# Conditioning sums on VectorE, a reordered layer head, and causal attention outputs with the values as stationary operand

## The chip, the core and the metric

The kernel runs on one core of one Trainium2 chip. The metric is the device time of one execution in microseconds, lower is better. The core's engines are TensorE (PE, its weight loads PEld), VectorE (DVE), ScalarE (ACT), GpSimd (POOL) and SyncE (SP), which here issues the weight DMAs.

## The reference

One sequence of 256 positions and 1024 channels passes two blocks. The first has two transformer layers conditioned on a vector `c` (a matrix-vector product with `ada_w`, six vectors of 1024 each layer), with differential attention, neighbourhood attention and a convolutional feed-forward network. The second has two hybrid layers, and most of the change is there:

```python
def hybrid_layer(x, ...):
    h = rmsnorm_2(x, norm_g)
    proj = h @ w_in                       # nsa_q, nsa_kv, pool_in, conv_in, fox_qkv, gates, merges ...
    o_nsa = nsa_mixer(...)                # gated sum of compressed, selected and window attention, 4 heads of 64
    o_pool = pool_mixer(...)
    o_conv = conv_mixer(...)
    o_fox = fox_mixer(...)                # causal attention with a decay from a cumulative sum, 4 heads of 64
    for i, o in enumerate((o_nsa, o_pool, o_conv, o_fox)):
        branch = (o * silu(gates[:, :, i])) @ w_branch[i]
        acc += sigmoid(merge[:, :, i]) * branch
    return x + acc @ w_out
```

With 256 positions, the selection takes every block and the window covers all keys, so the selected and the window parts are plain causal attention over different keys.

## The kernel before

**Weights.** All weights pass one queue of units of up to 1 MB. SP loads a unit into one of three slots of `RAW` (`load_unit`). ACT makes its high part (`split_hi`, L526), DVE or POOL its low part (`split_lo`/`lo_prep`, L536), and TensorE multiplies in three products (L554 to L556; L963 to L965, L970 and L971, L918 to L924 with activations stationary). `NH`/`NL` (NHL in the trace) hold the parts of the normed input, `WHL` those of the weights. PE, DVE, ACT, POOL and SP each run their own instruction list, written out by hand, and meet through semaphores.

**Conditioning.** A unit of `ada_w` is 128 rows by 2048 columns and isn't split: `pe_ada` (L568) multiplies it in float32 with a stationary operand of 32 columns (`CB`, which holds silu(c) and silu(c_ctx)), four matmuls beside each other on four column groups. Each float32 matmul is two recorded passes, so a unit shows as x8. Blocks 0 to 7 of units are named `("ada", b, k)`. Block 4 goes another way: DVE adds its eight units up, each times its element of `c`, in `WSUM` (`dve_ada_step`, L579), and TensorE sums over the partitions once (`pe_ada_joint`, L586).

**Hybrid layer.** `pe_layer` is the order on PE: `pe_head` (norm and the first projections, among them the values `va`, `vb`), the up projections of the compression, the gate projections g1, g2, g0, g3 with `pe_compress_sum` (L2116) and the first score jobs between, and then the causal attention in six jobs i = 0 to 5 (`CAUSAL`: fox, queries 0 to 127 and 128 to 255; then the two NSA kinds likewise). A job goes: `pe_causal_qk` scores (L2205, L2206, L2208), DVE mask and maximum (L2221, L2225, L2228), ACT exponential with row sums (L2253), DVE reciprocal r (L2234) and for NSA r times the gate (L2238), PE transpose (`pe_causal_turn`, L2273), ACT copy (L2283), `pe_causal_pv` (L2298), and DVE scaling by r into `OF` or `ON` (`dve_causal_out`, L2310). A projection of about 5.8 us stands between a job's steps on PE. At the end `pe_turn_nsa` and `pe_turn_fox` transpose `ON` and `OF` (L2602, L2615), and DVE multiplies by the gate `G` (`dve_gated`, L2431).

**Head.** `dve_turn_product` is a lane shuffle (L1957) and a multiplication by the rotary table (L1959); L2051 is the cumulative sum of the decay, on which ACT's `act_decay` (L2004, L2006) waits.

Of the kernel before, what the change touches and what calls it, by code (L numbers as in the profile page):

```python
# [13 lines left out]
P = 128  # L14
# [123 lines left out]
UP_ADA = {("up", 0, 0): (0, 1, 2, 3), ("up", 0, 2): (4,), ("up", 0, 3): (5,), ("up", 0, 4): (6,), ("up", 0, 5): (7,)}  # L138
QKV_ADA = {("qkv", 1, 4): (0, 1, 2), ("qkv", 1, 5): (3,)}
JOINT_ADA = {("up", 0, HALF_FT + 1): (7,)}  # L140
# [9 lines left out]
def unit_orders():  # L150
# [32 lines left out]
    for j in range(HALF_FT):  # L183
        add(("up", 0, j), 2)
        for k in {1: range(4), 2: (4,), 3: (5,), 4: (6,), 5: (7,)}.get(j, ()):
            add_ada(3, k)
# [109 lines left out]


# [67 lines left out]
def bass_two_block_decoder(nc, wstream, first, small, consts, late, rpb, xin, out):  # L365
    ctx = ExitStack()
    with ctx:
# [47 lines left out]
        QN, KN, KC, QF, KF, CBG, ON, OF = (  # L415
            sb(n, [P, 2, 256]) for n in ("QN", "KN", "KC", "QF", "KF", "CBG", "ON", "OF"))
# [53 lines left out]
        c_silu, c_zero, lam_v, lam_exp = (sem(n) for n in ("c_silu", "c_zero", "lam_v", "lam_exp"))  # L470
# [101 lines left out]
        def dve_ada_step(e, k):  # L572
            v = UNIT_OF["ada", 4, k]
            e.wait_ge(d_raw[v % 3], 16 * (v // 3 + 1))
            if k == 0:
                e.tensor_scalar(WSUM[:, :], RAW[:, v % 3, :], CB[:, k, 0:1], None, ALU.mult).then_inc(ada_acc, 1)
                return
            e.wait_ge(ada_acc, k)
            e.scalar_tensor_tensor(out=WSUM[:, :], in0=RAW[:, v % 3, :], scalar=CB[:, k, 0:1], in1=WSUM[:, :],  # L579
                                   op0=ALU.mult, op1=ALU.add).then_inc(ada_acc, 1)  # L580

        def pe_ada_joint(e):
            e.wait_ge(ada_par, 3)
            e.wait_ge(ada_acc, 8)
            for j in range(4):
                mm = e.matmul(AB[32 * j:32 * j + 32, :], ONE.to_broadcast([P, 32]), WSUM[:, 512 * j:512 * j + 512],  # L586
                              start=True, stop=True)
# [341 lines left out]
        def pe_wide(e, key, outs, T, xh, xl, wait_x):  # L929
# [3 lines left out]
            for j, o in enumerate(outs):  # L933
# [655 lines left out]
        def pe_ffn(e, l):  # L1589
            T, ring = (512, 3) if l == 0 else (256, 6)  # L1590
            for c, js in chunks(l):
                for jj, j in enumerate(js):
# [6 lines left out]
                    if l == 0 and c == 0:  # L1599
                        for k in UP_ADA.get(("up", 0, jj), ()):  # L1600
                            if k > 1:
                                pe_ada(e, 3, k)
                        if jj == 9:
                            pe_ada_turn(e, 3)
                    if l == 0 and c == 1 and jj == 1:
                        pe_ada_joint(e)
# [242 lines left out]
        def pe_proj(e, l, name):  # L1849
            pe_ring_free(e, l, name)  # L1850
# [1519 lines left out]
```

## Time and profile before

| | |
|---|---|
| median of 3 runs | 1594.96 us (1594.63 to 1595.36) |
| the profiled execution | 1595.22 us, its span 1593.4 us |
| mean granted clock of TensorE | 0.997 |
| PE / PEld busy | 98% / 82% |
| DVE / ACT / POOL busy | 59% / 47% / 34% |
| first hybrid layer, second | about 1075 to 1330 us, 1330 to 1582 us |

The span is what the profile covers; the rest of the execution's 1595.22 us, 1.8 us, lies around it. A row of a timeline gives start, duration, engine, line, operation and operands; rows that follow each other closely are joined as xN, and a matmul's duration reaches past the start of the next one, so the cost of matmuls is read from start to start.

### The profile page before, as it was taken

The page shows a single profiled execution, that of the slowest core. Times are in us where ns is not written, and L with a number is a line of the kernel's source. Part 1 is how long each engine was busy: PE and PEld are TensorE (multiplying, and loading weights), DVE is VectorE, ACT ScalarE, POOL GpSimd, SP SyncE. Part 2 cuts the span into 40 slices and gives each one's busy share as a digit, 9 for nine tenths or more (in the row PEclk, how much of TensorE's full clock was granted, in tenths as well). Part 3 has the DMA queues.
Part 4 walks back from the last instruction along what each step waited for, and adds up shares of the span by engine and source line. Part 5 has one row for each costly group of instructions (what it writes and reads, how often), then busy time and mean ns, then how long its engine had stood idle before and what let it go on. Part 6 is the DMA issues. An engine that isn't in the chain of part 4 may idle for free.

```text
span 1593.4 us, 23097 instructions
## 1 busy us (share of the span) xinstructions
PE 1568.6 (98%) x9146; PEld 1303.4 (82%) x9146; DVE 936.4 (59%) x1441; ACT 750.5 (47%) x1360; POOL 543.3 (34%) x354
## 2 busy tenths in 40 slices
PE   8999999999999999999999999999999999999998
PEld 5778557778887888879768899989998889998887
DVE  4434485555575554342266888757876457968435
ACT  5324485444322433243375755445654445654444
POOL 2224243322211222212273111007424657623663
PEclk9999999999999999999999999999999999999999
DMA  9264500534174222364313754454534534633551
GB/s 393 94 246 187 212 30 9 204 135 157 63 268 184 80 81 73 124 207 164 123 37 113 267 192 172 162 190 170 183 133 161 199 143 171 215 133 132 185 211 54
DMA packets 52603, 249.17 MB, mean 156 GB/s; under 512 B 20624, under 2 KB 21008, under 8 KB 26256
## 3 DMA queue, kind: packets, MB, share of 16 engines
q1 hardware_dynamic: 43744, 243.90, 42.2%
q10 hardware_dynamic: 8752, 3.80, 1.0%
q8 instruction: 73, 1.20, 0.3%
q14 instruction: 34, 0.28, 0.0%
HBM read 246.63 MB, written 1.05 MB: 155 GB/s over the span
## 4 chain that ended last, share of the span: by engine, by line
PE 88%; DVE 5%; ACT 3%; issue 1%; DMA 1%; POOL 1%; SPq 0%; POOLq 0%; ACTq 0%; DVEq 0%
PE psq L554 16%; PE psq L555 16%; PE psq L556 16%; PE ps L554 7%; PE ps L556 7%; PE ps L555 7%; PE psq L970 3%; PE ps L568 1%; PE psq L971 1%; PE ps L970 1%; DMA RAW<-wstream 1%; ACT WHL L526 1%; PE psq L1365 1%; PE ps L1393 1%; PE psq L2298 1%
## 5 line engine op out<-in xcount | busy, mean ns | idle before, releaser
L536 DVE TENSOR_TENSOR WHL<-RAW,WHL 128x1024 fp32r<-128x1024 f32 (+3 forms) x264 | 324.9, 1254 | 290.1 <-ACT WHL L526 289.6
L536 POOL TENSOR_TENSOR WHL<-RAW,WHL 128x1024 fp32r<-128x1024 f32 (+2 forms) x116 | 304.5, 2627 | 504.6 <-ACT WHL L526 471.8
L526 ACT ACTIVATE WHL<-RAW 128x1024 fp32r<-128x1024 f32 (+2 forms) x380 | 361.4, 1002 | 196.1 <-DMA RAW<-wstream 98.6
L554 PE MATMUL psq<-NHL,WHL 128*128 128x256 f32 (+1 forms) x1072 | 353.8, 330 | 1.7 <-POOL WHL L536 0.7
L555 PE MATMUL psq<-NHL,WHL 128*128 128x256 f32 (+1 forms) x1072 | 349.0, 326 | 0.0
L556 PE MATMUL psq<-NHL,WHL 128*128 128x256 f32 (+1 forms) x1072 | 348.9, 325 | 0.0
L554 PEld LDWEIGHTS psq<-NHL,WHL 128*128 128x128 f32 x1072 | 205.2, 191 | 28.9 <-issue 7.5
L556 PEld LDWEIGHTS psq<-NHL,WHL 128*128 128x128 f32 x1072 | 205.3, 191 | 16.6
L555 PEld LDWEIGHTS psq<-NHL,WHL 128*128 128x128 f32 x1072 | 205.3, 191 | 15.4
L554 PE MATMUL psq<-WHL,NHL 128*128 128x512 f32 (+1 forms) x320 | 124.8, 390 | 1.7 <-DVE WHL L536 1.7
L556 PE MATMUL psq<-WHL,NHL 128*128 128x512 f32 (+1 forms) x320 | 123.3, 385 | 0.0
L555 PE MATMUL psq<-WHL,NHL 128*128 128x512 f32 (+1 forms) x320 | 123.2, 385 | 0.0
L554 PE MATMUL ps<-NHL,WHL 128*128 128x512 f32 (+1 forms) x272 | 94.9, 349 | 0.0
L555 PE MATMUL ps<-NHL,WHL 128*128 128x512 f32 (+1 forms) x272 | 94.1, 346 | 0.0
L556 PE MATMUL ps<-NHL,WHL 128*128 128x512 f32 (+1 forms) x272 | 94.0, 346 | 0.0
L1716 DVE SCALAR_TENSOR_TENSOR TMP<-psq,SMALL,TMP 128x510 f32<-128x510 f32 (+1 forms) x64 | 39.2, 613 | 79.7 <-ACT TMP L1677 79.7
L699 ACT ACTIVATE TMP<-X 128x256 f32<-128x256 f32 (+1 forms) x52 | 25.1, 498 | 120.7 <-DVE X L1532 59.9
L1677 ACT ACTIVATE TMP<-psq,SMALL 128x512 f32<-128x512 f32 (+1 forms) x64 | 40.8, 666 | 87.0 <-PE psq L556 87.0
L554 PEld LDWEIGHTS psq<-WHL,NHL 128*128 128x128 f32 x320 | 60.1, 188 | 14.3 <-DVE WHL L536 2.1
L556 PEld LDWEIGHTS psq<-WHL,NHL 128*128 128x128 f32 x320 | 60.1, 188 | 11.5
L555 PEld LDWEIGHTS psq<-WHL,NHL 128*128 128x128 f32 x320 | 60.1, 188 | 11.0
L1752 POOL TENSOR_TENSOR HL<-TMP,HH 128x512 fp32r<-128x512 f32 x22 | 28.8, 1308 | 112.9 <-ACT HH L1663 112.9
(389 smaller groups left out, 2975.6 us busy)
## 6 DMA issues: line engine op xcount, KB each, us to landing
RAW<-wstream SPq DMA_DIRECT2D x194, 1024.0 KB, 4.8
RAW<-wstream SPq DMA_DIRECT2D x32, 704.0 KB, 4.0
K<-first SPq DMA_DIRECT2D x4, 1024.0 KB, 17.2
RAW<-wstream SPq DMA_DIRECT2D x4, 800.0 KB, 4.3
X<-xin SPq DMA_DIRECT2D x2, 1024.0 KB, 6.1
V<-first SPq DMA_DIRECT2D x2, 1024.0 KB, 19.3
Q<-first SPq DMA_DIRECT2D x2, 1024.0 KB, 24.7
BR<-rpb ACTq DMA_DIRECT2D x8, 256.0 KB, 8.2
```

The costliest lines, as they stand in the source:

```text
L526: e.activation(WH[:, u % 3, a:z], RAW[:, v % 3, a:z], ACT.Copy).then_inc(w_hi, 1)
L536: e.tensor_tensor(WL[:, u % 3, a:z], RAW[:, v % 3, a:z], WH[:, u % 3, a:z].bitcast(F32), ALU.subtract).then_inc(w_lo_p if pool else w_lo_v, 1)
L554: e.matmul(o, lh, rh, start=start, stop=False)
L555: e.matmul(o, lh, rl, start=False, stop=False)
L556: return e.matmul(o, ll, rh, start=False, stop=stop)
L568: mm = e.matmul(AB[32 * j:32 * j + 32, :], CB[:, c, :], RAW[:, v % 3, 512 * j:512 * j + 512], start=k == 0, stop=k == ada_units(b) - 1)
L699: e.activation(sq_tile(n, m), X[:, m, 0:NORM_T[n]], ACT.Square).then_inc(x_sq, 1)
L970: e.matmul(o[:, 0:512], wh, x, start=start, stop=False, skip_group_check=True)
L971: return e.matmul(o[:, 0:256], wl, x[:, 0, :], start=False, stop=stop, skip_group_check=True)
L1677: e.activation(acc_tile(l, U, s), up_banks(l, jj)[s][:, :], ACT.Identity, scale=small_at("fconv", (3 * l + 1) * 44 + j + FT * s), bias=sma ...
L1716: e.scalar_tensor_tensor(out=a3[:, :, 1:256], in0=o3[:, :, 0:255], scalar=w(0), in1=a3[:, :, 1:256], op0=ALU.mult, op1=ALU.add).then_inc(u ...
L1752: e.tensor_tensor(HL[l][:, jj, :], acc_tile(l, U, 0), HH[l][:, jj, :].bitcast(F32), ALU.subtract).then_inc(h_lo, 1)
```

## The change

1. **Conditioning.** Units 4 to 7 of block 3 are no longer multiplied on PE. DVE sums them for both vectors (`WSUM` gets two planes), in steps ahead of up projections 1, 3, 5 and 7, and `pe_ada_joint(3)` multiplies the two sums before up 8. Their loads follow up 2, 4, 6 and 8 instead of 2 to 5. Unit (5, 3) is multiplied before qkv 4 of layer 1 and not before qkv 5. `CB` is cleared by POOL and not by DVE.
2. **Head.** DVE's split of the first value unit (`lo_prep(qn)`) moves into the norm, after its step m = 3. The shuffle of `dve_turn_product` stands apart from its product, and the product now follows the split of the first g1 unit. ACT's copy to `KF` follows that unit's high part. The first half of g2 stands ahead of `pe_causal_qk(0)`, the second behind it.
3. **Causal outputs.** DVE scales P by r ahead of the transpose (`dve_causal_scale`), `pe_causal_turn` waits for that. `pe_causal_pv` has the values as stationary operand, 64 columns on the left or right column half of PE, and P^T moves: the result is already transposed. NSA's kinds and the compressed part are summed in one bank by accumulation. `ON`, `OF`, their transposes and the scaling of outputs go away.
4. **Gating.** `dve_fox_gated` reads the fox result ahead of `dve_pool_sums`, `dve_nsa_gated` after conv's taps; `conv_u` stands ahead of `cmp_weigh(0)`, and r of the compressed part is multiplied by its gate.

```diff
-UP_ADA = {("up", 0, 0): (0, 1, 2, 3), ("up", 0, 2): (4,), ("up", 0, 3): (5,), ("up", 0, 4): (6,), ("up", 0, 5): (7,)}
-QKV_ADA = {("qkv", 1, 4): (0, 1, 2), ("qkv", 1, 5): (3,)}
+UP_ADA = {("up", 0, 0): (0, 1, 2, 3)}
+UP_SUMMED = {1: 4, 3: 5, 5: 6, 7: 7}
+QKV_ADA = {("qkv", 1, 4): (0, 1, 2, 3)}
...
+            for c, t in enumerate(sums):
...
+                e.scalar_tensor_tensor(out=t, in0=RAW[:, v % 3, :], scalar=CB[:, k, c:c + 1], in1=t,
+                                       op0=ALU.mult, op1=ALU.add).then_inc(ada_acc, 1)
...
+        def dve_causal_scale(e, l, i):
...
+            for g, tile in enumerate(p_tiles(qt)):
+                p = TMP[:, tile, :].rearrange("p (l k) -> p l k", l=2)
+                e.tensor_tensor(p, p, r[:, g, :].unsqueeze(2).to_broadcast([P, 2, 256]), ALU.mult).then_inc(p_scaled, 1)
...
         def pe_causal_pv(e, l, i):
...
-            o = bank[2][:, 256 * (i % 2):256 * (i % 2) + 256]
-            for n, h in enumerate(HEADS):
-                for k in range(qt + 1):
-                    c = ((n % per) * (qt + 1) + k) * P
-                    v = VF[:, k, 64 * h:64 * h + 64] if kind == 2 else VN[:, k, 64 * kind:64 * kind + 64]
-                    mm = e.matmul(o[:, 64 * h:64 * h + 64], TMP[:, t_tiles(qt)[n // per], c:c + P], v, start=k == 0,
-                                  stop=k == qt)
+            if i == 2:
+                e.wait_ge(z_mul, z_value(l, 3))
+            for k in range(qt + 1):
+                for a in range(2 if kind == 2 else 1):
+                    for par in range(2):
+                        half = slice(64 * par, 64 * par + 64)
+                        o = bank[2][half, :].rearrange("p (c q) -> p c q", c=2)[:, :, qt * P:qt * P + P]
+                        t = TMP[:, t_tiles(qt)[par if qt else 0], :].rearrange("p (n q) -> p n q", n=4)
+                        t = t[:, k:4:2, :] if qt else t[:, 2 * par:2 * par + 2, :]
+                        if kind == 2:
+                            v, o, t = VF[:, k, 128 * a + 64 * par:128 * a + 64 * par + 64], o[:, a, :], t[:, a, :]
+                        else:
+                            v = VN[:, k, 64 * kind:64 * kind + 64]
+                        mm = e.matmul(o, v, t, start=i in (0, 2) and k + a == 0, stop=kind == 2 and k == qt,
+                                      skip_group_check=True)
...
@@ pe_layer @@
             pe_compress_sum(e, l)
+            pe_proj(e, l, "g2", (0,))
             pe_causal_qk(e, l, 0)
-            pe_gates(e, l, 2)
+            pe_proj(e, l, "g2", (1,))
```

In the order on DVE the head of a hybrid layer reads before, from the split of the last compression unit on:

```order
L536 TENSOR_TENSOR WHL<-RAW,WHL 128x1024 [waits w_hi]
L1957 STREAM_SHUFFLE TMP<-TMP 128x512 [waits raw_copy]
L1959 TENSOR_TENSOR TMP<-TMP,LATEC 128x512 [waits nrot_v]
L536 TENSOR_TENSOR WHL<-RAW,WHL 128x1024 [waits w_hi]
L2051 SCALAR_TENSOR_TENSOR TMP<-CONST,psq 128x256 [waits fx_tr]
L1966 TENSOR_TENSOR QN<-QN,TMP 128x512 [waits nrot_c,nrot_v]
```

And now (L548 is the split, L1986 the shuffle, L1992 the product, L2083 the cumulative sum):

```order
L548 TENSOR_TENSOR WHL<-RAW,WHL 128x1024 [waits w_hi]
L1986 STREAM_SHUFFLE TMP<-TMP 128x512 [waits raw_copy]
L548 TENSOR_TENSOR WHL<-RAW,WHL 128x1024 [waits w_hi]
L1992 TENSOR_TENSOR TMP<-TMP,LATEC 128x512 [waits nrot_v]
L2083 SCALAR_TENSOR_TENSOR TMP<-CONST,psq 128x256 [waits fx_tr]
L1999 TENSOR_TENSOR QN<-QN,TMP 128x512 [waits nrot_c,nrot_v]
```

The split of the first g1 unit has passed the product, and the product stands directly ahead of the cumulative sum. On DVE around the two jobs that precede the pool's sums (L2459) it read before:

```order
L536 TENSOR_TENSOR WHL<-RAW,WHL 128x1024 [waits w_hi]
L2234 RECIPROCAL STAT<-STAT 128x4 [waits att_exp]
L2238 TENSOR_TENSOR STAT<-STAT,CM 128x4 [waits att_r,gs_v]
L2310 TENSOR_TENSOR OF<-psq,STAT 128x256 [waits att_r,att_pv]
L2221 TENSOR_TENSOR psq<-psq,LATEC 128x512 [waits att_qk]
L2225 TENSOR_REDUCE STAT<-psq 128x2x2 [waits att_mask]
L536 TENSOR_TENSOR WHL<-RAW,WHL 128x1024 [waits w_hi]
L2459 TENSOR_TENSOR PU<-PU 128x2x256 [waits pads,sb_copy]
```

And now (L2270 and L2274 are r, L2291 the scaling, L2257 and L2261 mask and maximum, L2460 the gating, L2488 the pool's sums):

```order
L548 TENSOR_TENSOR WHL<-RAW,WHL 128x1024 [waits w_hi]
L2270 RECIPROCAL STAT<-STAT 128x4 [waits att_exp]
L2274 TENSOR_TENSOR STAT<-STAT,CM 128x4 [waits att_r,gs_v]
L2291 TENSOR_TENSOR TMP<-TMP,STAT 128x512 [waits att_r]
L2291 TENSOR_TENSOR TMP<-TMP,STAT 128x512
L2257 TENSOR_TENSOR psq<-psq,LATEC 128x512 [waits att_qk]
L2261 TENSOR_REDUCE STAT<-psq 128x2x2 [waits att_mask]
L548 TENSOR_TENSOR WHL<-RAW,WHL 128x1024 [waits w_hi]
L2460 TENSOR_TENSOR TMP<-psq,G 128x512 [waits g_v,att_pv]
L2488 TENSOR_TENSOR PU<-PU 128x2x256 [waits pads,sb_copy]
```

The output scaling of a job became two scalings of P of twice the width, on which the job's transposes wait, and a gating that waits for the second fox output stands ahead of the pool's sums.

## Rows read from the trace of the kernel before

**Rows 1.** The page, busy time of each engine over the span.
```profile
PE 1568.6 (98%) x9146; PEld 1303.4 (82%) x9146; DVE 936.4 (59%) x1441; ACT 750.5 (47%) x1360; POOL 543.3 (34%) x354
```

**Rows 2.** Timeline of the weight loads in the head, layer 0.
```profile
1094.03 0.19 PEld L965 LDWEIGHTS psq<-NHL,WHL 128*128 128x128 f32 x1
1095.26 0.19 PEld L554 LDWEIGHTS psq<-WHL,NHL 128*128 128x128 f32 x1 [1.03 <-DVE WHL L536]
```

**Rows 3.** Timeline of PE where projection g1 changes halves.
```profile
1121.22 0.28 PE L556 MATMUL psq<-NHL,WHL 128*128 128x256 f32 x1
1121.98 0.39 PE L554 MATMUL psq<-NHL,WHL 128*128 128x256 f32 x1 [0.48 <-POOL WHL L536]
```

**Rows 4.** Timeline of DVE in the head, layer 0.
```profile
1091.07 1.94 DVE L867 TENSOR_TENSOR NHL<-TMP,NHL 128x256 fp32r<-128x256 f32 x1 [1.20 <-ACT NHL L849]
...
1094.22 0.98 DVE L536 TENSOR_TENSOR WHL<-RAW,WHL 128x800 fp32r<-128x800 f32 x1
...
1116.42 2.12 DVE L1959 TENSOR_TENSOR TMP<-TMP,LATEC 128x512 f32<-128x512 f32 x1
```

**Rows 5.** Timeline of PE around the compression's sums and causal_qk(0).
```profile
1126.49 1.06 PE L2116 MATMUL ps<-CONST,TMP 32*128 32x16 f32 x8
...
1129.82 0.41 PE L556 MATMUL psq<-NHL,WHL 128*128 128x256 f32 x1
1130.04 0.41 PE L554 MATMUL psq<-NHL,WHL 128*128 128x256 f32 x1
...
1132.59 0.28 PE L554 MATMUL psq<-NHL,WHL 128*128 128x256 f32 x1
1132.71 0.28 PE L555 MATMUL psq<-NHL,WHL 128*128 128x256 f32 x1
```

**Rows 6.** Windows there and in the second layer: busy us, granted clock, DMA share, GB/s.
```profile
1130.00:1135.00 5.00, 5.00 (x35) 5.00 (x34) 4.63 (x11) 0.34 (x2) 0.56 (x1) 0.74 0.74 251
1385.00:1390.00 5.00, 5.00 (x32) 5.00 (x31) 4.41 (x10) 0.36 (x2) 0.54 (x1) 0.66 0.69 247
```

**Rows 7.** Timeline of PE, causal outputs of job 1.
```profile
1168.51 1.90 PE L2298 MATMUL psq<-VNF,TMP 128*128 128x64 f32 x16
1170.24 1.04 PE L2273 MATMUL ps<-CONST,TMP 128*128 128x128 f32 x8
```

**Rows 8.** Timeline of PE, attention of the layer before; half-width stationaries.
```profile
809.95 1.09 PE L1393 MATMUL ps<-TMP,V 128*64 128x128 f32 x16
810.98 1.13 PE L1365 MATMUL psq<-K,Q 64*128 64x512 f32 x4
```

**Rows 9.** Timeline of PE, one conditioning unit of block 3.
```profile
367.77 0.39 PE L556 MATMUL psq<-NHL,WHL 128*128 128x512 f32 x1
368.08 1.07 PE L568 MATMUL ps<-RAW,CB 128*32 128x512 f32 x8
369.08 0.50 PE L554 MATMUL ps<-NHL,WHL 128*128 128x512 f32 x1
369.42 0.39 PE L555 MATMUL ps<-NHL,WHL 128*128 128x512 f32 x1
```

**Rows 10.** Source view of the running weight sums.
```profile
L579 DVE SCALAR_TENSOR_TENSOR WSUM<-RAW,CB,WSUM x7: 2345/2349/3192, 440.2 to 482.4; 128x2048 f32<-128x2048 f32 x7
```

**Rows 11.** Timeline of PE, output transposes.
```profile
1249.92 0.60 PE L2602 MATMUL psq<-CONST,ON 128*128 128x128 f32 x4
1250.27 0.48 PE L554 MATMUL psq<-WHL,NHL 128*128 128x512 f32 x1
```

**Rows 12.** Timeline of PE at the next layer's first projection.
```profile
686.42 1.06 PE L568 MATMUL ps<-RAW,CB 128*32 128x512 f32 x8
688.17 0.47 PE L918 MATMUL psq<-NHL,WHL 128*128 128x512 f32 x1 [0.69 <-ACT NHL L851]
```

**Rows 13.** Timeline of DVE between two causal jobs.
```profile
1162.06 2.06 DVE L2238 TENSOR_TENSOR STAT<-STAT,CM 128x4 f32<-128x4 f32 x1
...
1165.10 0.69 DVE L2225 TENSOR_REDUCE STAT<-psq 128x4 f32<-128x512 f32 x1
```

More of the change, by code:

```diff
@@ L184, in unit_orders @@
         add(("up", 0, j), 2)
-        for k in {1: range(4), 2: (4,), 3: (5,), 4: (6,), 5: (7,)}.get(j, ()):
+        for k in {1: range(4), 2: (4,), 4: (5,), 6: (6,), 8: (7,)}.get(j, ()):
             add_ada(3, k)
@@ L231, in unit_orders @@
             runs[r:r] = [("ada", b, k) for k in ks]
+    for key, b in JOINT_AT.items():
+        r = runs.index(key)
+        runs[r:r] = [("joint", b)]
     return keys, every, runs
@@ L295, in product_end @@
     return GEMM_BEFORE[KEYS[v]] + unit_products(KEYS[v])
+ADA_ACC = {}
+acc_count = 0
+for b_, ks_ in SUMMED.items():
+    for k_ in ks_:
+        acc_count += 1 if b_ == 4 else 2
+        ADA_ACC["ada", b_, k_] = acc_count
 SPLIT_UNITS = [v for v, k_ in enumerate(KEYS) if k_[0] != "ada"]
@@ L582, in pe_ada_joint, with weight_sums, dve_ada_step @@
[L582 to L587, printed above, removed]
+        def weight_sums(b):
+            return [WSUM[:, c, :] for c in range(1 if b == 4 else 2)]
+        def dve_ada_step(e, b, k):
+            v = UNIT_OF["ada", b, k]
+            sums = weight_sums(b)
+            at = ADA_ACC["ada", b, k] - len(sums)
+            e.wait_ge(d_raw[v % 3], 16 * (v // 3 + 1))
+            if b == 4 and k == 0:
+                e.wait_ge(gemm, product(("joint", 3)))
+            for c, t in enumerate(sums):
+                if k == SUMMED[b][0]:
+                    e.tensor_scalar(t, RAW[:, v % 3, :], CB[:, k, c:c + 1], None, ALU.mult).then_inc(ada_acc, 1)
+                    continue
+                e.wait_ge(ada_acc, at - len(sums) + c + 1)
+                e.scalar_tensor_tensor(out=t, in0=RAW[:, v % 3, :], scalar=CB[:, k, c:c + 1], in1=t,
+                                       op0=ALU.mult, op1=ALU.add).then_inc(ada_acc, 1)
@@ new lines, in bass_two_block_decoder, with pe_ada_joint @@
+        CBF = CB[:, :, :].rearrange("p k n -> p (k n)")
+        ONE_AT = (CBF[:, 16:48], CBF[:, 15:47])
+        def pe_ada_joint(e, b):
+            if b == 4:
+                e.wait_ge(ada_par, 3)
+            e.wait_ge(ada_acc, ADA_ACC["ada", b, SUMMED[b][-1]])
+            for c, t in enumerate(weight_sums(b)):
+                for j in range(4):
+                    mm = e.matmul(AB[32 * j:32 * j + 32, :], ONE_AT[c], t[:, 512 * j:512 * j + 512], start=b == 4,
+                                  stop=b == 4 or c == 1)
@@ L588, in pe_ada_joint @@
             mm.then_inc(gemm, 1)
         def act_ada_row(e, b):
-            e.wait_ge(gemm, product(("ada", b, ada_units(b) - 1)))
+            e.wait_ge(gemm, product(("joint", b) if b in SUMMED else ("ada", b, ada_units(b) - 1)))
             if b >= 2:
@@ L1599, in pe_ffn @@
                     if l == 0 and c == 0:
-                        for k in UP_ADA.get(("up", 0, jj), ()):
-                            if k > 1:
-                                pe_ada(e, 3, k)
+                        if jj == 0:
+                            pe_ada(e, 3, 2)
+                            pe_ada(e, 3, 3)
+                        if jj == 8:
+                            pe_ada_joint(e, 3)
                         if jj == 9:
@@ L1707, in dve_ffn @@
                     U, key = 22 * l + j, ("up", l, j)
+                    if l == 0 and j in UP_SUMMED:
+                        dve_ada_step(e, 3, UP_SUMMED[j])
                     split_lo(e, ahead(key), False)
@@ L2379, in act_cmp_turn, with pe_cmp_pv @@
             e.activation(TMP[:, 6, 128 * qt:128 * qt + P], bank[6 + qt][:, 0:P], ACT.Copy).then_inc(att_pt, 1)
-        def pe_cmp_pv(e, l, qt):
-            e.wait_ge(att_pt, TR_BASE + 11 * l + 10 + qt)
-            e.matmul(bank[3 + qt][:, 0:256], TMP[:, 6, 128 * qt:128 * qt + P], VCB, start=True,
-                     stop=True).then_inc(att_pv, 1)
-        def dve_cmp_out(e, l, qt):
-            x = TMP[:, 8 + qt, 256:512]
-            g = GS[:, qt, 0:4].unsqueeze(2).to_broadcast([P, 4, 64])
-            e.wait_ge(att_pv, PV_BASE + 8 * l + 7 + qt)
-            e.wait_ge(gs_v, l + 1)
-            e.tensor_tensor(x.rearrange("p (h d) -> p h d", h=4),
-                            bank[3 + qt][:, 0:256].rearrange("p (h d) -> p h d", h=4), g, ALU.mult).then_inc(att_o, 1)
-            e.wait_ge(att_o, O_BASE + 8 * l + 6 + 2 * qt)
-            e.wait_ge(nsa_o, 4 * l + 2 * qt + 1)
-            e.tensor_tensor(ON[:, qt, :], ON[:, qt, :], x, ALU.add).then_inc(nsa_o, 1)
+        def pe_cmp_pv(e, l):
+            e.wait_ge(att_pt, TR_BASE + 11 * l + 11)
+            for c in range(2):
+                mm = e.matmul(bank[2][:, 256 * c:256 * c + 256], VCB[:, P * c:P * c + P], TMP[:, 6, 0:256], start=False,
+                              stop=True, skip_group_check=True)
+            mm.then_inc(att_pv, 1)
         GATE_ORDER = (1, 2, 0, 3)
@@ L2890, in act_layer @@
             act_causal_exp(e, l, 5)
+            act_gated(e, l, 3, FOX_Z)
             act_conv_b(e, l)
```

192 lines of the change are left out of this document (79 added, 113 removed).

## The prediction

> **What bounds the kernel.** I read the page's busy times first: PE works 98% of the span, 24.8 of 1593.4 us are left over, and DVE, ACT and POOL are far from full [rows 1]. So an edit gains by passes taken off PE, by closing one of PE's few gaps, or by the clock, and work given to another engine costs nothing unless PE comes to wait for it. Then I read the timelines where the change puts its hand. PE stands in the head of a hybrid layer for the low half of the first value unit: one weight load starts at 1094.03, the next at 1095.26, where 0.12 us is usual, 1.1 us lost; DVE's split, for which it waits, starts only at 1094.22 [rows 2, 4]. PE stands again in g1, for POOL's half of the split: 1121.22 to 1121.98, 0.64 us over a step [rows 3]. The clock is the third place. Behind the compression's sums and the first scores the projection matmuls start 0.22 us apart, at 1132.59 the step is 0.12 again, and the windows grant 0.74 and 0.66 [rows 5, 6]. Those are the two levels, 1.2 and 2.4 GHz. What PE did just before, from 1126.49 on, is matmuls with 32 or 64 rows and few columns [rows 5].
>
> **Conditioning.** Four units leave PE. One takes 1.00 us to the next start, and the changes of form around it cost 0.31 and 0.34 us where two 512-column steps take some 0.23 each: 0.19 more, 1.19 in all [rows 9]. 4 x 1.19 = 4.8 us go. The joint product has twice a unit's passes, 2 x 1.00, with the changes once: about 2.1. Gain 2.7 us. On DVE come eight operations of 128x2048 at 2.35 us [rows 10], 19 us in four up steps' pairs, while DVE works 59% of the span [rows 1]; the low splits queued behind them are made ahead of their products. I take nothing for this; if cover were missing at each of the four steps, each would cost up to its 4.7 us less the slack of a unit, so I allow 0 to 4 us. Unit (5, 3) fills a wait: PE stands from the end of the first three units, 687.48, to 688.17 [rows 12]. It costs 1.19 where it stood, and about 0.7 of its time falls into the wait, so I take 0.5, with 0 to 0.9 as bounds, since its weights may land late there. Clearing `CB` is nothing: its first matmul waits for data.
>
> **Head.** The value split of 0.98 us goes ahead of a norm step where DVE waited 1.20 us [rows 4]; it fits, and up to 1.1 us of the gap closes if ACT's half has come by then. In g1 the high part comes one copy earlier, about 0.5 us, which covers most of the 0.64. Against it stands the cumulative sum: before, the split lay between the product and the sum, so that the product (1116.42, 2.12 us) was long done. Now the product stands after the split and directly ahead of the sum. Beside POOL's split it took 2.12 us, where a reduction of 128x512 takes 0.69 [rows 4, 13]. The sum may start up to 2 us later, ACT's decay, the g2 split and the copy for `compress_sum` with it. I take 0.6 us gained for each layer, 1.2 in all, bounds -0.5 and 1.5 each. The Trainium skill, "SBUF — State Buffer", section "SBUF: two separate sides", says that a DVE operation with two SBUF inputs and a GpSimd one that reads SBUF lock each other out for a whole instruction; the 2.12 us agree. By it each moved product could double the loss, and it is why I don't take the full 1.5.
>
> **Clock.** With g2's first half, 24 dense matmuls of 0.12 us, 2.9 us, between the 16-column sums and the 64-row scores [rows 5], the two thin stretches no longer join. The loss is read from the windows: 0.34 x 5 = 1.7 us in the second layer; in the first the slow steps reach from 1129.82 at the latest to 1132.59, at least 2.8 us at half clock, so 1.4 or more, and I take 1.7 there too [rows 5, 6]. Gain 3.4 us if the dips go, 0 if they stay.
>
> **Causal outputs.** Before, 16 passes take 1.73 us, 0.108 each [rows 7]; a layer has 3 jobs of 8 and 3 of 16, 72 passes, 7.8 us, 15.6 in both. After, fox has 24 passes of 128 columns on half-width stationaries. The nearest row has just this form: 16 passes in 1.03 us, 0.064 each [rows 8], less than the 0.108 of one that has the array alone, so the halves run side by side. 24 x 0.064 = 1.55 us. The NSA kinds have 24 passes of 256 columns. Two steps of four 512-column passes take 1.00 us [rows 9], so a step of 256 columns 0.25, and a pair of halves as much: 12 x 0.25 = 3.0 us. Entering the narrow form costs 0.08 [rows 9] for each of six jobs, 0.5. Together 5.1 us a layer; gain 2.7, for both 5.4. Bounds: if a step ran at half of four-abreast, twice as long, the NSA part would lose 3.0 more a layer (the rival below), and if leaving the form were free it would gain 1 more for both. The 16 transposes go: 0.35 us for four [rows 11], and about 0.1 for the change of form, as behind the conditioning unit [rows 9]: 4 x 0.43 = 1.7 us.
>
> The first stands against a rule. The Trainium skill, "TensorE: Matmul & The Clock Gate", section "The mechanism", says that weight loads overlap matmuls in flight only where row groups differ, and here both halves use all rows. By it each pair would run one after the other, and the gain of 5.4 would be a loss. The trace has the pairing with all 128 rows [rows 8] and contradicts it, so I follow the row.
>
> **Scaling of P.** New on DVE: nine 128x512 operations a layer, two in a job of 256 keys, on the path exponential, r, scale, transpose, copy, output. Their nearest rows are 0.69 us for 512 columns of DVE [rows 13] and 2.12 for a product beside POOL [rows 4]. Job 1: r's second operation runs 1162.06 to 1164.12 [rows 13], the transposes start at 1170.24 [rows 7]. Two scalings end between 1165.5 and 1168.4. That leaves 1.8 us or more, so I take nothing. Queued behind them are mask and maximum, which ended at 1165.79 [rows 13] and would end at 1170 in the bad case; the exponential and the next scaling then still have a projection and more ahead of them. The output scalings, which left, and `conv_u` ahead of the weighing I price at nothing.
>
> **Sum.** 2.7 + 0.5 + 1.2 + 3.4 + 5.4 + 1.7 = 14.9 us. From the profiled execution's own 1595.2 that is 1580.3; the median of the runs is 0.3 lower, so I forecast 1580.0.
>
> **Rivals.**
> *The half clock stays*, at the same place or behind g2's second half: the thin matmuls are all still there, and only their spacing changed. For it speaks that the scores still follow each other in one piece; against it that every job has such scores and the span's mean grant of 0.997 leaves 4.8 us for all dips, of which these two are 3.4. 1580.0 + 3.4 = 1583.4.
> *The halves don't pair* at 256 columns or in accumulation in one bank: each NSA pass costs 0.22 and not 0.125, 24 x 0.1 x 2 layers = 4.6 more, and 0.108 for fox, 2.1 more: 1586.7. Against it stand [rows 8].
> *DVE comes late in the head*: the cumulative sum's delay reaches `compress_sum`, and the gains in the head turn into a loss of 1 to 2 us a layer: 1583 to 1585.
> *Slower than before*: the scalings at 2.1 us each, with masks and low splits behind them, push the exponential past the next job's slack, so that PE waits at the transposes. It decides once job 1's scalings end 1.8 us later than the bad case above. To eat 15 us, the ten turns of jobs 1 to 5 of both layers must each wait 1.5 us; at 2 us each the kernel ends at 1600. Against it: DVE waits for ACT before these splits and has time between jobs.
>
> **Numbers.** My forecast has 0.5; the clock staying 0.2; DVE late in the head or a smaller new wait 0.15; halves unpaired 0.07; a larger gain, by terms at their upper bounds, 0.05; slower 0.03. The forecast's own range is 1577.5 to 1582; the whole runs from 1576.5 to 1586. What this measurement can tell from no change is 0.2%, 3.2 us. Only a heavy form of the DVE rivals or the last ends above 1591.8: faster 0.95, same 0.02, slower 0.03.
>
> **What would show it.** Causal outputs: 16 passes of 128 columns to the next start in 1.0 us, 8 passes of 256 columns in about 1.0. Windows behind g2 at 1.00. PE's gap for the value unit under 0.5 us, no gap at g1's second half, and none at the 16-column sums. No PE wait on DVE's scaling at a transpose. In the up projections of layer 0 no wait for DVE's low splits. I am wrong if a row of 0.5 us or more of PE idle names DVE scaling, DVE's weighted sums or the copy for the sums, or if half-clock steps of 0.21 us remain.

## The result, and the profile after

The changed kernel took 1597.84 us (median of 14 runs, 1595.97 to 1600.28), the kernel before beside it 1594.98 (14 runs). The ratio is 1.0016, with a 95% interval of 1.0009 to 1.0023: slower by 0.16%, where 1580.0 was forecast. That is 12 us above the top of the forecast range, 1576.5 to 1586. Its profiled execution has a span of 1596.9 us and a granted clock of 0.994.

The page, busy times and the chain that ended last, to be read against [rows 1]:

```profile
PE 1566.0 (98%) x9066; PEld 1295.0 (81%) x9066; DVE 951.3 (60%) x1446; ACT 748.7 (47%) x1360; POOL 536.7 (34%) x356
...
PE 80%; DVE 10%; ACT 5%; issue 2%; DMA 2%; POOL 0%; SPq 0%; ACTq 0%; POOLq 0%; DVEq 0%
```

PE's busy time is down by 2.6 us, with matmuls at half clock counted at their full length, and it is still busy 98% of a longer span. The chain says more: PE's share of it is 80%, DVE's 10 and ACT's 5, where before it was 88, 5 and 3. A timeline of PE in the first layer, outputs 1, 2 and 3 with the transposes of jobs 3, 4 and 5 behind them, for [rows 7], and then job 5's transposes in the second layer:

```profile
1164.53 1.09 PE L2352 MATMUL psq<-TMP,VNF 128*64 128x128 f32 x16
1165.55 1.09 PE L2322 MATMUL ps<-CONST,TMP 128*128 128x128 f32 x8
...
1173.59 0.65 PE L2352 MATMUL psq<-TMP,VNF 128*64 128x256 f32 x4
1175.88 0.66 PE L2322 MATMUL ps<-CONST,TMP 128*128 128x128 f32 x4 [1.65 <-DVE TMP L2287]
...
1186.62 1.08 PE L2352 MATMUL psq<-TMP,VNF 128*64 128x256 f32 x8
1187.63 1.09 PE L2322 MATMUL ps<-CONST,TMP 128*128 128x128 f32 x8
```

```profile
1444.12 1.97 PE L2322 MATMUL ps<-CONST,TMP 128*128 128x128 f32 x8 [2.68 <-DVE TMP L2291]
```

The matmul form does what was forecast: 16 passes of 128 columns take 1.02 us to the next start, for 1.73. Output 1 starts 4.0 us earlier than before, output 2 (before at 1178.12) begins 4.5 us earlier. Then PE stands 1.65 us for DVE's scaling of job 4 (L2287), in the second layer 1.63 us for job 4 and 2.68 us for job 5. Behind the stand at 1175 and the one at 1444 the clock is at its lower level, 1.2 GHz, for much of the time. The windows (us, busy time by engine, granted clock, DMA) answer [rows 6]:

```profile
1130.00:1135.00 5.00, 5.00 (x43) 4.53 (x42) 4.64 (x14) 2.25 (x10) 0.00 (x0) 1.00 0.62 210
1175.00:1180.00 5.00, 4.06 (x21) 3.76 (x22) 2.86 (x6) 3.01 (x10) 0.00 (x0) 0.72 0.38 159
1180.00:1185.00 5.00, 5.00 (x29) 5.00 (x29) 4.39 (x5) 2.40 (x4) 2.46 (x1) 0.60 0.00 0
1385.00:1390.00 5.00, 4.99 (x40) 4.70 (x42) 4.63 (x9) 0.23 (x1) 0.98 (x1) 1.00 0.67 252
1440.00:1445.00 5.00, 2.32 (x16) 1.59 (x15) 4.76 (x10) 0.00 (x0) 0.73 (x1) 0.84 0.59 210
1445.00:1450.00 5.00, 4.94 (x19) 4.11 (x18) 3.60 (x10) 3.11 (x5) 1.70 (x1) 0.50 0.01 3
1450.00:1455.00 5.00, 5.00 (x16) 3.96 (x15) 3.63 (x10) 2.15 (x3) 1.60 (x3) 0.63 0.56 208
```

At the old places, 1130 and 1385, the clock is now full. At the new ones it is 0.72, 0.60, 0.84, 0.50 and 0.63. What is missing to 1, times 5 us, comes to 3.4 us in the first layer and 5.1 in the second, the most that this can have cost. The timeline of DVE in the first layer, for [rows 13]:

```profile
1161.99 2.10 DVE L2274 TENSOR_TENSOR STAT<-STAT,CM 128x4 f32<-128x4 f32 x1
1164.12 1.29 DVE L2291 TENSOR_TENSOR TMP<-TMP,STAT 128x512 f32<-128x512 f32 x2
...
1166.06 0.69 DVE L2261 TENSOR_REDUCE STAT<-psq 128x4 f32<-128x512 f32 x1
1169.33 1.23 DVE L548 TENSOR_TENSOR WHL<-RAW,WHL 128x1024 fp32r<-128x1024 f32 x1 [2.58 <-ACT WHL L538]
...
1171.07 2.31 DVE L2488 TENSOR_TENSOR PU<-PU 128x512 f32<-128x512 f32 x1
...
1175.14 0.69 DVE L2287 TENSOR_TENSOR TMP<-TMP,STAT 128x512 f32<-128x512 f32 x1
```

The low split (L548) that DVE made at 1168.36 before it makes at 1169.33 now, though PE is 4 us ahead, and job 4's scaling comes at 1175.14. Where the lead went is read from output 3. Rows of the kernel before, transposes of job 4, output 3 and transposes of job 5:

```profile
1178.96 0.61 PE L2273 MATMUL ps<-CONST,TMP 128*128 128x128 f32 x4
...
1186.57 1.90 PE L2298 MATMUL psq<-VNF,TMP 128*128 128x64 f32 x16
1188.30 1.04 PE L2273 MATMUL ps<-CONST,TMP 128*128 128x128 f32 x8
```

Output 3 starts at 1186.62 now, 0.05 us later than before. Of the 4.5 us of lead the wait for the scaling took about 1.5, the half clock behind it the other 3. The chain of waits between 1155 and 1190, first of the kernel before, then of the changed one, shares by line:

```profile
by line: PE psq L554 22.9%; PE psq L556 21.2%; PE psq L555 21.2%; PE psq L2298 14.7%; PE ps L2273 7.6%; PE psq L2208 3.9%; PE psq L2331 3.3%; PE ps L2208 3.0%; PE ps L2331 2.4%; issue 0.4%
```

```profile
by line: ACT TMP L2302 12.8%; ACT WHL L538 11.2%; DVE STAT L2274 10.5%; issue 8.9%; DVE TMP L2291 7.4%; DVE WHL L548 7.1%; DVE X L2499 7.1%; DVE PU L2488 6.4%; DVE STAT L2264 4.0%; DVE TMP L2287 4.0%; DVE ps L2257 2.0%; DVE X L2503 2.0%; DV
```

Before, every piece of it is PE, but for 0.4% of issue. Now it runs ACT exponential (L2302), ACT high part (L538), DVE low split (L548), the pool's sums and means (L2488, L2499), r and gate (L2274), scaling (L2291), mask and maximum, and the next exponential. None of its 106 pieces is PE's: in this stretch the loop closed without a wait for PE.

### The profile page after: what moved, and what is told of

The parts are those of the page before. It is cut to its first block, busy times and chain, and to the rows that moved or that the text cites. A ratio compares the mean times of both kernels' runs of the same rounds, so it can differ in the third digit from the quotient of the medians.

```text
span 1596.9 us, 22916 instructions
## 1 busy us (share of the span) xinstructions
PE 1566.0 (98%) x9066; PEld 1295.0 (81%) x9066; DVE 951.3 (60%) x1446; ACT 748.7 (47%) x1360; POOL 536.7 (34%) x356
## 4 chain that ended last, share of the span: by engine, by line
PE 80%; DVE 10%; ACT 5%; issue 2%; DMA 2%; POOL 0%; SPq 0%; ACTq 0%; POOLq 0%; DVEq 0%
PE psq L566 14%; PE psq L568 14%; PE psq L567 14%; PE ps L566 7%; PE ps L568 7%; PE ps L567 7%; PE psq L996 3%; DMA RAW<-wstream 2%; DVE WHL L548 2%; ACT WHL L538 2%; PE psq L997 1%; PE ps L996 1%; PE ps L580 1%; PE psq L1391 1%; ACT TMP L2302 1%
## 5 line engine op out<-in xcount | busy, mean ns | idle before, releaser
L548 DVE TENSOR_TENSOR WHL<-RAW,WHL 128x1024 fp32r<-128x1024 f32 (+3 forms) x264 | 333.8, 1288 | 295.5 <-ACT WHL L538 294.5
L548 POOL TENSOR_TENSOR WHL<-RAW,WHL 128x1024 fp32r<-128x1024 f32 (+2 forms) x116 | 298.2, 2573 | 503.9 <-ACT WHL L538 471.1
L538 ACT ACTIVATE WHL<-RAW 128x1024 fp32r<-128x1024 f32 (+2 forms) x380 | 361.2, 1002 | 190.7 <-DMA RAW<-wstream 88.2
```

What stands on the lines that cost most here:

```text
L538: e.activation(WH[:, u % 3, a:z], RAW[:, v % 3, a:z], ACT.Copy).then_inc(w_hi, 1)
L548: e.tensor_tensor(WL[:, u % 3, a:z], RAW[:, v % 3, a:z], WH[:, u % 3, a:z].bitcast(F32), ALU.subtract).then_inc(w_lo_p if pool else w_lo_v, 1)
```

## The experiments

Medians, and the ratio to the kernel before beside them with its interval. Before was 1595.33 to 1595.87 in these comparisons. The intervals are some 2 us wide to either side, so the order of e8 to e15 among themselves is mostly inside them; what is said of it rests on the profiles, one for each kernel.

| kernel | us | ratio |
|---|---|---|
| e1 no causal part | 1597.82 | 1.0009 (1.0000 to 1.0017) |
| e2 causal part alone | 1599.63 | 1.0029 (1.0018 to 1.0040) |
| e3 pool's sums later | 1594.93 | 0.9997 (0.9988 to 1.0006) |
| e4 low splits later | 1585.32 | 0.9935 (0.9923 to 0.9948) |
| e5 before, low splits later | 1593.26 | 0.9984 (0.9975 to 0.9992) |
| e6 e1, low splits later | 1588.20 | 0.9953 (0.9940 to 0.9967) |
| e7 waits filled | 1598.78 | 1.0022 (1.0013 to 1.0030) |
| e8 e4, g2 whole | 1584.97 | 0.9934 (0.9922 to 0.9947) |
| e9 e4, two more moves | 1583.82 | 0.9926 (0.9913 to 0.9938) |
| e10 e9, g2 whole | 1583.78 | 0.9925 (0.9913 to 0.9937) |
| e11 e4, no conditioning part | 1588.11 | 0.9953 (0.9940 to 0.9967) |
| e12 e4, no head part | 1583.06 | 0.9922 (0.9910 to 0.9935) |
| e13 e12, value split moved | 1582.99 | 0.9918 (0.9905 to 0.9932) |
| e14 e12, copy and product moved | 1586.63 | 0.9941 (0.9928 to 0.9953) |
| e15 e13, conv_u moved | 1582.70 | 0.9913 (0.9899 to 0.9926) |

**e1: the causal part undone.** The changed kernel with the parts 3 and 4 of the diff taken back.

> The kernel before with the conditioning and head parts alone, causal outputs and gating as before. Theory A (PE, now ahead, waits for DVE's scaling at the turns of jobs 4 and 5, and the stall brings the half clock): the trace of after is 3.1 us ahead at the start of the hybrid layers, and about 1.0 and 1.6 us more are gained up to the first turn of each layer, so 1594.98 - 5.7 = about 1589.3, half-clock stretches at most where before had them. Rival B (the earlier parts only moved waits and give nothing): 1594 to 1595. Rival C (DVE and ACT are the bound of the causal stretch anyway, so that even without scaling PE's lead is lost there): 1591 to 1593.

The median of 1597.82 is above all three forecasts. In mechanism it is C: PE is 4.7 us ahead of the kernel before at output 2, and by 1197 all is gone. The waits of PE, us in total, times, longest:

```profile
PE psq L2335 <- DVE ON L2350: 2.8, 2, 1.9
...
PE psq L567 <- DVE CXY L2551: 2.4, 2, 1.2
```

There is no scaling of P here. PE waits for the old scaling of outputs (`ON`) and for `CXY`, and behind these waits the window at 1190 has a clock of 0.66. So the lead is lost to DVE without the new scaling, and the scaling is not the only cause.

**e2: the causal part alone.**

> The kernel before with the new causal outputs and gating alone. Theory A: PE reaches job 4's turn about 4 us later than in the changed kernel, while DVE's scaling comes at the same time, so the waits are gone or under 0.5 us and no half clock follows; the form of the matmuls and the transposes that went give 2 to 5 us: 1590 to 1593. Rival D (the new matmul form itself brings waits or the half clock): slower than before by 3 us or more, with half-clock stretches behind the outputs.

Theory A's sum missed. The waits for DVE's scaling are there although PE lacks the 3 us of the conditioning part:

```profile
PE ps L2285 <- DVE TMP L2254: 3.9, 2, 2.7
...
PE ps L2285 <- DVE TMP L2250: 1.7, 2, 1.1
```

No half clock stands behind the first scores. In the first layer it follows the wait of 2.67 us at job 5, in the second one of only 0.57 us at job 4 (0.75 at 1435). In number, and in its dips, this is rival D; that the form alone doesn't bring the half clock only e4 shows, which has the form and full clock. I had taken the lead as the cause; the loop had also become longer. From one low split to the next, around job 3, DVE took 7.72 us in the kernel before and 8.76 in the changed one.

**e3: the pool's sums behind job 5's maximum.**

```diff
             dve_fox_gated(e, l)
-            dve_pool_sums(e, l)
             dve_causal_r(e, l, 4)
             dve_causal_scale(e, l, 4)
             dve_causal_max(e, l, 5)
+            dve_pool_sums(e, l)
```

> The changed kernel with the pool's sums on DVE moved behind the scaling and the maximum of jobs 4 and 5. Theory A: the wait of 1.65 us at job 4's turn in each layer goes, and with it the half clock behind it in the first layer (some 3 us); in the second layer the wait at job 5 shrinks: 1588 to 1592. Rival D (the form of the matmuls brings the half clock): the waits go, 3.3 us, but the dips stay: about 1594 to 1595. Rival C: the time saved comes back as a wait at job 5, 1596 or more.

The wait at job 4 went. One of 2.1 us stands at job 5 in each layer, with the half clock behind it: part of what was taken came back one job later, as C had it. The 1594.93 falls into D's range, but D had these waits gone.

**e4: the low splits behind the maximum.**

```diff
             dve_causal_max(e, l, 3)
-            lo_prep(e, l, "pool", False)
             dve_causal_r(e, l, 3)
             dve_causal_scale(e, l, 3)
             dve_causal_max(e, l, 4)
-            lo_prep(e, l, "conv_x", False)
+            lo_prep(e, l, "pool", False)
             dve_fox_gated(e, l)
-            dve_pool_sums(e, l)
             dve_causal_r(e, l, 4)
             dve_causal_scale(e, l, 4)
             dve_causal_max(e, l, 5)
+            lo_prep(e, l, "conv_x", False)
+            dve_pool_sums(e, l)
+            dve_causal_r(e, l, 5)
+            dve_causal_scale(e, l, 5)
             lo_prep(e, l, "conv_b", False)
             dve_pool_means(e, l)
-            dve_causal_r(e, l, 5)
-            dve_causal_scale(e, l, 5)
```

> As e3, and DVE's low splits of the pool, conv_x and conv_b units also stand behind scaling and maximum of their job, so that DVE no longer waits for ACT's high part between a job's exponential and its scaling. Theory A, with the DVE and ACT ping-pong as the cause: scaling ends some 3 us earlier in each job, no wait at any turn, no dip: 1585 to 1588. If the low splits were what PE needs next, a wait for them appears at the projections and the time is no better than e3.

As expected, 12.5 us below the changed kernel, by order alone. Timelines of DVE, of POOL, and of PE at output 2:

```profile
1167.53 2.14 DVE L2274 TENSOR_TENSOR STAT<-STAT,CM 128x4 f32<-128x4 f32 x1
1169.71 0.69 DVE L2287 TENSOR_TENSOR TMP<-TMP,STAT 128x512 f32<-128x512 f32 x1
...
1172.45 1.22 DVE L548 TENSOR_TENSOR WHL<-RAW,WHL 128x1024 fp32r<-128x1024 f32 x1
...
1176.22 3.38 DVE L2291 TENSOR_TENSOR TMP<-TMP,STAT 128x512 f32<-128x512 f32 x2 [0.23 <-DVE STAT L2274]
```

```profile
1176.07 2.37 POOL L548 TENSOR_TENSOR WHL<-RAW,WHL 128x1024 fp32r<-128x1024 f32 x1 [6.42 <-ACT WHL L538]
```

```profile
1174.57 0.65 PE L2352 MATMUL psq<-TMP,VNF 128*64 128x256 f32 x4
1175.15 0.66 PE L2322 MATMUL ps<-CONST,TMP 128*128 128x128 f32 x4
```

Job 4's scaling ends at 1170.4, 4.7 us ahead of the transposes, and the low split at 1172.45 finds ACT's high part ready. Two scalings of job 5, started beside POOL's low split of 1176.07, take 3.38 us instead of 1.29, 2.1 more, and still nobody waits. The Trainium skill, in "SBUF — State Buffer", section "SBUF: two separate sides", has a lock between a DVE operation with two SBUF inputs and a GpSimd one that reads SBUF; the trace agrees: the pair ends at 1179.60, 1.16 us after POOL's end at 1178.44, about the 1.29 us that it takes alone.

**e5 and e6: the same order without the new outputs.** e5 is the kernel before, e6 is e1, both with reciprocal and maximum of jobs 2 to 5 ahead of the low splits.

> The kernel before with DVE's order alone changed as in e4: reciprocal and maximum of jobs 2 to 5 ahead of the low splits of the pool, conv_x and conv_b units. Theory A (before, PE and the DVE-ACT chain of these jobs are about level, PE sets the end): nothing to gain while PE carries its old work, 1594.5 to 1595.5, no wait of PE gone that was there. Rival E (the order by itself is worth most of e4's gain): 1588 to 1591.

> e1 (conditioning and head parts, old causal outputs) with the order of e4 on DVE. Theory A: in e1 PE was 4.7 us ahead before the waits on ON and CXY and lost all; with the order it keeps it in both layers: 1594.98 - 3.1 - 1.0 - 1.6 - up to 1 of the half clock = 1588.5 to 1589.5; e4 stands 3 to 5 us below it, and that is what the matmul form and the transposes give. Rival C (the chain is as long without the order): no better than e1.

e6 is A's case to 0.3 us, with e4 2.9 us below it instead of 3 to 5. e5 gained 2.1 us where A said nothing. Its profile has only one of before's two half-clock stretches behind the scores (about 1.5 us), and its PE timeline agrees with that of before to 0.36 us up to 1211. Its runs step with the granted clock: 1592.0 to 1592.5 us at 1.000, 1593.2 to 1593.6 at 0.998 and 0.999, 1594.5 and 1595.1 at 0.997. The kernel before gets nothing from a higher clock: beside e5, its five runs at 0.999 took 1595.05 to 1595.46, its four fastest, at 0.998, 1594.55 to 1594.80. So the order alone is worth 0.4 us on PE's timeline and up to 2.1 in the time, where more clock comes with it (why is open), and 10 to 12 us once PE is faster (e1 to e6, and the changed kernel to e4). The new outputs are worth e6 less e4, 2.9 us.

**e7: PE's waits filled.** 12 dense matmuls ahead of the wait at job 4, 20 at job 5 of the second layer.

```diff
+            fill = 12 if i == 4 else 20 if i == 5 and l else 0
+            if fill:
+                e.wait_ge(att_pt, base)
+                for n in range(fill):
+                    e.matmul(bank[6][:, 0:256], NH[:, n % DT, 0:P], NH[:, n % DT, 0:256], start=True, stop=True)
```

> The changed kernel with dense matmuls of 128 rows and 256 columns, whose result nobody reads, put in front of PE's wait for the scaled P: 12 at job 4's turn in both layers, 20 at job 5's in the second. Theory H (PE's idle stretch, followed by thin matmuls, brings the half clock): the half-clock stretches at 1175 to 1185 and 1440 to 1455 go, worth 3.4 + 5.1 us, and the waits' own time stays: 1589 to 1592. Rival I (the thin matmuls alone bring it): dips as in the changed kernel, 1597 to 1600.

The time missed H and fell into I's range, while the windows are H's:

```profile
1175.00:1180.00 5.00, 4.93 (x39) 4.44 (x38) 2.77 (x6) 3.09 (x10) 0.00 (x0) 1.00 0.36 151
1180.00:1185.00 5.00, 4.62 (x39) 3.88 (x37) 4.47 (x5) 2.32 (x4) 2.49 (x1) 1.00 0.07 8
1190.00:1195.00 5.00, 4.94 (x15) 4.05 (x15) 4.35 (x11) 2.36 (x4) 2.49 (x2) 0.50 0.06 10
1445.00:1450.00 5.00, 4.85 (x33) 3.81 (x31) 3.53 (x11) 1.49 (x3) 0.00 (x0) 1.00 0.43 177
```

```profile
1187.30 1.11 PE L2327 MATMUL ps<-CONST,TMP 128*128 128x128 f32 x4 [2.68 <-DVE TMP L2291]
```

At 1175, 1180 and 1445, where the fill is, the clock is full, and the second layer's causal stretch takes 2.4 us less. In the first layer PE now reaches job 5 at full speed and waits there 2.68 us, where I had put no fill; behind that wait the clock is 0.50, and this layer's stretch takes 2.5 us more. Half clock on PE had given DVE time to catch up. Taking it away up to job 5 moved the wait and gained nothing: the transposes of job 5 start at 1187.30 where they started at 1187.63. Up to there the loop sets the time; behind job 5 the clock counts as well.

**e8: g2 whole again, on e4.**

> e4 with both halves of projection g2 behind causal_qk(0), as before the change. Theory J (the prediction's term: the spacing keeps the clock): half-clock windows come back after the first scores, 1.7 us in each layer, so e4 + 2 to 4 us: 1587.5 to 1589. Rival K (the dips depend on something else that is gone too): same as e4 within 1 us.

Both half-true. The half clock is back in both layers:

```profile
1125.00:1130.00 5.00, 5.00 (x31) 4.89 (x31) 4.96 (x5) 1.59 (x3) 2.37 (x1) 0.68 0.62 213
1375.00:1380.00 5.00, 4.94 (x31) 4.73 (x31) 4.97 (x4) 3.11 (x5) 3.75 (x2) 0.74 0.47 159
```

And the time is e4's. In the first layer the stretch from the sums to job 0's transposes takes 17.9 us in e4 and 18.0 in e8. Splitting g2 brings two more changes of form (6.4 us of g2 for 5.86), and PE, being faster, meets this in e4:

```profile
1141.05 0.66 PE L2322 MATMUL ps<-CONST,TMP 128*128 128x128 f32 x4 [0.55 <-DVE TMP L2287]
```

**e9 and e10: two more moves, with g2 in halves and whole.** Job 0's r and scaling stand ahead of `dve_gates(2)`, and `conv_u` ahead of the low split of `conv_c`.

> e4 with two more moves on DVE: reciprocal and scaling of job 0 ahead of the low split of the g2 unit's follower, and conv_u ahead of the low split of conv_c. In e4 PE waited 0.57 us at job 0's turn in the first layer, and about 0.46 and 0.4 us for CXY. Theory A: these go, e4 less 1.0 to 1.5 us: 1583.8 to 1584.5. If the moved splits become late instead, no gain.

> e9 with g2 whole behind causal_qk(0). In e8 the half clock came back (1.7 us a layer), and the whole took no longer, since the split of g2 had cost two changes of form (0.55 us a layer) and a wait at job 0's turn (0.7 and 0.2 us). With that wait gone in both kernels, the split should now pay: this one 1 to 2.5 us slower than e9. If the half clock's cost is hidden by something else still, equal.

e9 met A. In its trace the wait at job 0 is gone and one of 1.5 us at job 1's transposes, for ACT's copy, has come. e10 pays for its half clock and waits there only 0.7 us: equal again, against my expectation.

**e11 and e12: conditioning, and head, undone on e4.**

> e4 with the conditioning as before. From the traces PE was 3.1 us ahead at the first hybrid layer through it: e4 + 2.7 to 3.3 us, 1588 to 1588.6. If part of it were hidden elsewhere, less than 2 us.

> e4 with the head as before: value split, product order, KF copy, g2 whole. Seen in the traces: the value unit's gap of 1.0 us returns in both layers, the half clock of 1.7 us too, against changes of form and a wait of together 0.75 to 1.25 us a layer: e4 + 2.5 to 3.5 us: 1587.8 to 1588.8. If the head moves gained only the value gap: e4 + 2.

The conditioning part is worth 2.8 us, as expected. Without the head part I had expected 2.5 to 3.5 us more, and e12 is 2.3 us faster than e4. The stretch from the sums to job 0's transposes takes 16.2 us in both layers of its trace, where e4 takes 17.9 and 17.3, which is more than the value unit's gap of 1.0 us costs. Two windows of e12, whose like is half slow in e8:

```profile
1125.00:1130.00 5.00, 4.94 (x41) 4.73 (x41) 4.71 (x8) 0.42 (x2) 2.48 (x1) 1.00 0.75 233
1375.00:1380.00 5.00, 4.94 (x41) 4.73 (x41) 4.88 (x6) 0.60 (x3) 2.72 (x1) 1.00 0.66 215
```

The matmuls behind the scores are those of the kernel before, in its order, and here they ran at full clock in both layers. In e8, with the same order of matmuls there, both layers have the half clock and the stretch takes 18.0 and 17.9 us. So e12 owes much to a clock that g2 in one piece does not always get. And from e5 to e6, where conditioning and head come together, the gain is 5.1 us, 2.3 more than conditioning's 2.8. What the head part is worth in time stays open, between these 2.3 us of gain and 2.3 of loss.

**e13 to e15: what of the head helps.**

> e12 (no head moves, no half clock in its trace) with one of them: DVE's split of the value unit inside the norm. In e4, e8, e9 and e10 this closed a gap of 1.0 us in each layer. If it does here and nothing else changes: e12 - 2.0 = 1581.1. If closing that gap is what brings the half clock behind the first scores (e8 and e10 have it, e12 has not): half-clock windows behind the scores and 1583 to 1584.5.

> e12 with the other head moves but g2's split: the copy to KF behind the high part of g1, and the rotary product behind the low split of g1. From e8 against e12 these took 0.4 us off g1's wait and gave 0.3 back at the 16-column sums and 0.4 ahead of it: 0 to 0.5 us of gain, 1582.6 to 1583.1. If the late product is what costs in e4: 1584 or more, with PE waiting at the sums or at job 0.

> e13 with conv_u ahead of the low split of conv_c, which took a wait of 0.16 us in e12 and 0.7 us in e4 off PE: e13 less 0.1 to 0.5 us, the fastest of all kernels here if e13 is at 1581.

Moving the value split takes 0.6 us a layer off PE's timeline. The windows of e13 show the half clock in the first layer, not in the second:

```profile
1125.00:1130.00 5.00, 5.00 (x31) 4.93 (x30) 4.67 (x9) 0.23 (x1) 1.78 (x1) 0.66 0.63 218
1375.00:1380.00 5.00, 4.94 (x40) 4.73 (x40) 4.94 (x6) 0.63 (x3) 2.70 (x1) 1.00 0.61 210
```

Its runs are 1581.28, 1582.99, 1583.00 and 1584.49 at granted clocks of 1.000, 0.999, 0.998 and 0.997: steps of 1.5 to 1.7 us, about one half-clock stretch each. e15's are 1581.25, 1581.40, 1582.70, 1582.80 and 1582.86. e14 gains 0.6 us up to the sums, loses 0.3 at them, has two half-clock stretches and a wait for CXY, and is the slowest of the three. e15 has the lowest median, 0.87% below the kernel before, but e12, e13 and e15 lie within 0.4 us of each other and are not told apart.

## Why the prediction was wrong

**The step that failed** stands under "Scaling of P": "Two scalings end between 1165.5 and 1168.4. That leaves 1.8 us or more, so I take nothing." The scaling itself kept to it: r's gate took 2.10 us, two scalings 1.29, and they ended at 1165.4 (these are job 3's, whose transposes stand behind output 1; the prediction calls them job 1's) [rows 13]. What failed was the other side of the subtraction. I set DVE's time against the moment at which PE arrived before, 1170.24, and the same text moved that moment by 2.7 + 0.5 + 0.6 + 1.7 = 5.5 us up to there, outputs not counted. It moved by 4.7, to 1165.55, which left 0.14 us of the slack. DVE's and ACT's loop did not move along, since nothing in it waited for PE. Each microsecond taken off PE ahead of job 4 used up slack. The kernel before had 4.9 us of it at job 4, r's end at 1174.1 against the transposes at 1178.96, and 3.6 at job 5, 1184.7 against 1188.30:

```profile
1173.92 0.16 DVE L2238 TENSOR_TENSOR STAT<-STAT,CM 128x4 f32<-128x4 f32 x1
...
1184.52 0.16 DVE L2238 TENSOR_TENSOR STAT<-STAT,CM 128x4 f32<-128x4 f32 x1
```

Priced at nothing, the hand-over cost 6.0 us of waits (job 4 in both layers, job 5 in the second) and up to 8.5 us of half clock behind them, and e4, which has neither there, is 12.5 us faster. The prediction's own sign of being wrong, a wait of 0.5 us or more for DVE's scaling, stands in the trace four times, at job 0 (0.55 us) too. That PE works 98% of the span was true, and said nothing of how far the next bound lay.

**The rival** "slower than before" named the right engine, and its time of 1600 came nearest. It priced the scalings as slow operations (2.1 us); 16 of 18 took 0.69, and only job 0's, with 2.10 and 1.79 us, were slow. The cause was their place, behind a low split that waits for ACT, and e1 shows that the rest of the loop lost PE's lead without them. I gave it 0.03.

**Conditioning**: 2.7 and 0.5 forecast. PE is 3.1 us ahead at the first hybrid layer, and e11 against e4 gives 2.8. DVE's sums cost nobody a wait in the up projections; they took 2.35 us each, as priced:

```profile
L599 DVE SCALAR_TENSOR_TENSOR WSUM<-RAW,CB,WSUM x13: 2343/2345/3192, 345.6 to 480.2; 128x2048 f32<-128x2048 f32 x13
```

The fourth unit of the next layer's group waits 0.39 us for its load, then the projection follows without the gap of [rows 12]:

```profile
685.72 1.06 PE L580 MATMUL ps<-RAW,CB 128*32 128x512 f32 x8 [0.39 <-DMA RAW<-wstream]
686.72 0.50 PE L943 MATMUL psq<-NHL,WHL 128*128 128x512 f32 x1
```

**Causal outputs**: right in the passes. A layer's six outputs take 4.8 us for 7.7, and six entries into the narrow form 0.5 more, which show in the last step of the projection ahead (a projection takes 5.95 us instead of 5.85). That is 2.4 gained where 2.7 stood. The halves pair at 128 and at 256 columns. The Trainium skill's rule that I had set against [rows 8], in "TensorE: Matmul & The Clock Gate", section "The mechanism", is contradicted here too. The transposes gave 0.9 a layer. Of these 6.6 us for both layers e6 and e4 show 2.9 in the time. Four transposes behind a narrow output take 0.59 us instead of 0.54, eight 1.02 instead of 0.97, 0.6 in all, which was not in my sum. PE waits 0.7 us for CXY and 0.5 at job 0, where e6 waits for neither. In the profiles e4 also enters the hybrid layers 1.0 us later than e6, by waits in layers in which the two don't differ (one for ACT comes to 1.5 us in e4 and 0.4 in e6). The last 0.9 us I can't place.

**Head**: the value gap closed, as forecast. Weight loads of the changed kernel for [rows 2]:

```profile
1090.91 0.19 PEld L991 LDWEIGHTS psq<-NHL,WHL 128*128 128x128 f32 x1
1091.03 0.19 PEld L566 LDWEIGHTS psq<-WHL,NHL 128*128 128x128 f32 x1
```

Of 1.0 us, 0.4 came back in the next projections. The late product cost 0.28 us at the sums in the first layer. On PE's timeline the forecast of 0.6 a layer was of the right size; that it reached the time is not shown (e12).

**Clock**: 3.4 us forecast, and both stretches went. In the 16 places of the eight profiled kernels with g2 in halves the clock is full; with g2 whole it fell in 11 of 18. So the split does that, but the term of 3.4 us was mis-sized: e8 against e4 and e10 against e9 differ by 0.4 us or less. It costs changes of form, and PE at full clock waits for DVE or ACT soon after. Why the same order of matmuls falls to half clock in one layer of e13 and not in the other is open; I tried nothing on it.

## What to carry to other kernels

When an edit makes the busiest engine faster, measure the slack of every hand-over to it against its new time, not its old one, and follow the loop of the other engines for a turn: if no step in it waits for the fast engine, it will not come earlier. In such a loop, what only has to be ready later (here the low splits) goes behind what the next hand-over needs. A gain that vanishes is looked for in the chain of waits of the stretch, whose engine changes, while the busy share stays at 98%.

## What the runs showed of the hardware

Waits of PE of 1.65 and 2.68 us, followed by thin matmuls, were followed by half clock for some 5 to 10 us in the changed kernel, which cost more than the wait. Dense matmuls in the wait's place kept the clock full (e7). A wait's length alone doesn't tell: 0.57 us was followed by half clock in e2, 1.49 us in e9 was not. The granted clock differs between executions of one program, and the times step with it by 1 to 1.7 us (e5: 1.000 to 0.997, 1592.0 to 1595.1; e13 likewise), so differences below that need the profile's windows beside the times.
